# Attention blocks: V held in the array, P streaming for two heads on two column halves, row sums multiplied into the turned gate

## What is computed

```
for l in range(DEPTH):                       # DEPTH = 2
    u = rms_norm(x, g_pre[l]) @ w_in[l]
    (qa, ka, va, ga, qb, kb, vb, gb, rb, qm, gm) = split(u)
    oa = merge(moba_attention(q=8 heads of 64, k, v=va)) * silu(ga)   # causal, with ALiBi
    ob = merge(rms_norm(gla_attention(...), g_gla_out[l])) * silu(gb) # 4 heads, gated linear
    om = merge(mem_attention(q=4 heads of 64, mk, mv)) * silu(gm)     # 256 memory tokens
    x = x + concat([oa, ob, om]) @ w_out[l]
# mem_attention, and moba_attention for one block of 256 keys:
p = softmax(q @ k.T * scale + bias)          # 256 queries x 256 keys
o = p @ v                                    # 256 x 64 for each head
```

## Time and profile before

| | |
|---|---|
| median of 3 runs | 1408.54 us |
| profiled execution | 1409.29 us, span 1407.4 us |
| TensorE matmul busy | 1387.6 us, 99% |
| TensorE weight loads (beside matmuls) | 1142.5 us, 81% |
| VectorE busy | 1027.5 us, 73% |
| ScalarE busy | 1013.5 us, 72% |
| granted TensorE clock, mean | 0.999 |
| all DMA | 240.35 MB, 171 GB/s |

### The profile page before, as it was taken

One profiled execution on the slowest core, in us unless ns is written; L12 is line 12 of the kernel. 1 busy time (PEld: TensorE's weight loads), 2 busy tenths in 40 slices (PEclk: granted clock), 3 DMA queues, 4 the chain that ended last, 5 costly groups with the idle time before them and its releaser, 6 DMA issues.

```text
span 1407.4 us, 20632 instructions
## 1 busy us (share of the span) xinstructions
PE 1387.6 (99%) x7843; PEld 1142.5 (81%) x7843; DVE 1027.5 (73%) x1427; ACT 1013.5 (72%) x1838; POOL 74.8 (5%) x174
## 2 busy tenths in 40 slices
PE   7999999999999999999999999999999999999998
PEld 6788888888888888788887888887778888788886
DVE  5888788777666767776667766667988876876665
ACT  7657574748878555688785978767888886587784
POOL 8000000000000011000000000001120300000000
PEclk9999999999999999999999999999999999999999
DMA  7533453345656566556565656545453432566562
GB/s 233 192 120 94 150 194 122 119 150 181 202 186 205 181 227 209 184 191 204 184 202 172 202 187 198 191 154 194 144 149 123 110 123 91 168 209 203 185 206 91
DMA packets 168962, 240.35 MB, mean 171 GB/s; under 512 B 21714, under 2 KB 114800, under 8 KB 168864
## 3 DMA queue, kind: packets, MB, share of 16 engines
q1 hardware_dynamic: 166496, 233.57, 50.9%
q0 software_dynamic: 2336, 5.46, 1.4%
q10 hardware_dynamic: 32, 0.01, 0.0%
HBM read 236.12 MB, written 2.88 MB: 170 GB/s over the span
## 4 chain that ended last, share of the span: by engine, by line
PE 94%; DVE 2%; ACT 2%; DMA 1%; issue 0%; SPq 0%; ACTq 0%; DVEq 0%
PE A L261 18%; PE A L262 17%; PE A L263 17%; PE G L262 5%; PE M L262 5%; PE M L261 5%; PE M L263 5%; PE G L263 5%; PE G L261 5%; PE A L1349 1%; PE G L1270 1%; PE G L1317 1%; PE M L1327 1%; DMA block_cat<-in_mem 1%; DVE x_lo L439 1%; DVE tmp L434 1%
## 5 line engine op out<-in xcount | busy, mean ns | idle before, releaser
L243 DVE TENSOR_TENSOR w_lo<-raw,w_hi 128x1024 fp32r<-128x1024 f32 (+2 forms) x296 | 506.9, 1726 | 122.0 <-ACT w_hi L225 121.2
L225 ACT ACTIVATE w_hi<-raw 128x1024 fp32r<-128x1024 f32 (+2 forms) x296 | 427.2, 1462 | 116.1 <-DMA raw<-in_ffn_w_gate_up 86.9
L261 PE MATMUL A<-w_hi,x_hi 128*128 128x512 f32 (+1 forms) x640 | 258.2, 403 | 3.0 <-DVE x_lo L439 1.6
L263 PE MATMUL A<-w_hi,x_lo 128*128 128x512 f32 (+1 forms) x640 | 246.9, 386 | 0.0
L262 PE MATMUL A<-w_lo,x_hi 128*128 128x512 f32 (+1 forms) x640 | 246.8, 386 | 0.0
L714 ACT ACTIVATE ffn_ffn_hT<-ffn_ffn_hb 32x128 f32<-32x128 f32 x576 | 176.9, 307 | 15.7 <-DVE ffn_ffn_hb L779 2.5
L261 PEld LDWEIGHTS A<-w_hi,x_hi 128*128 128x128 f32 x640 | 120.3, 188 | 32.5 <-DVE x_lo L439 7.0
L263 PEld LDWEIGHTS A<-w_hi,x_lo 128*128 128x128 f32 x640 | 120.2, 188 | 25.1
L261 PE MATMUL A<-w_hi,ffn_ffn_hT_hi 128*128 128x512 f32 x352 | 138.1, 392 | 0.0
L262 PEld LDWEIGHTS A<-w_lo,x_hi 128*128 128x128 f32 x640 | 120.5, 188 | 21.0 <-issue 0.7
L262 PE MATMUL A<-w_lo,ffn_ffn_hT_hi 128*128 128x512 f32 x352 | 137.1, 389 | 0.0
(11 more groups left out here) (406 smaller groups left out, 2025.2 us busy)
## 6 DMA issues: line engine op xcount, KB each, us to landing
raw<-in_ffn_w_gate_up SPq DMA_DIRECT2D x176, 512.0 KB, 4.6
raw<-in_ffn_w_down SPq DMA_DIRECT2D x88, 512.0 KB, 3.9
raw<-in_w_in SPq DMA_DIRECT2D x48, 512.0 KB, 4.5
raw<-in_gdn_w_in SPq DMA_DIRECT2D x48, 512.0 KB, 4.5
raw<-in_sc_w_in SPq DMA_DIRECT2D x24, 512.0 KB, 4.5
raw<-in_w_out SPq DMA_DIRECT2D x16, 512.0 KB, 4.4
raw<-in_gdn_w_out SPq DMA_DIRECT2D x16, 512.0 KB, 4.0
raw<-in_w_mem_kv SPq DMA_DIRECT2D x8, 512.0 KB, 5.2
```

Of the source, the lines that this page charges most:

```text
L225: ins = act.activation(net.w_hi[:, v % RING, part], net.raw[:, v % RING, part], ACT.Copy)
L243: ins = dve.tensor_tensor(net.w_lo[:, v % RING, part], net.raw[:, v % RING, part], net.w_hi[:, v % RING, part].bitcast(F32), ALU.subtract)
L261: pe.matmul(out, xh, hi[:, k, c, :], start=start and k == 0, stop=False)
L263: mm = pe.matmul(out, xl, hi[:, k, c, :], start=False, stop=stop and k == nk - 1)
```

## The change

**P·V is turned round** (`pvp:n`, for heads n and n+1). V (128 keys x 64 columns) is now the stationary operand and PT streams, 256 tokens for the first 128 keys, and for the other 128 keys 128 tokens (causal heads) or 256 (memory heads). Head n uses the left 64 columns of the array, head n+1 the right 64 (`tile_position`), so O comes out transposed, features on the partitions, two heads in one 128-row block. `PT` gets four slots, which lie over QE and KE.

**The row sums go into the gate.** O can't be scaled by a row factor in this layout, so `jscale:g` multiplies the reciprocals into the gate, which still has tokens on the partitions; `gturn:g` transposes that part of the gate into a bank M. `ocopy:g` (ScalarE) copies O out of A[3] into the free part of `cat`, `join:g` (VectorE) multiplies it by the turned gate into `cT`, `join:g` on ScalarE copies the high part, `jlo:g` on VectorE the rest. `cturn` 0, 1 and 3 are gone, and three `gturn` come. Both tables are written anew around these steps.

```diff
-    unit:ga:0:3 pv:10 pturn:0 lo:16:0 join:1 hi:17:1 pv:11 scores:2 pturn:1 gate2:m
-    unit:ga:1:0 jgate:1
+    unit:ga:0:3 pturn:0 lo:16:0 hi:17:1 pvp:10 ocopy:1 scores:2 pturn:1 gate2:m
+    unit:ga:1:0 jscale:1
 ...
+        self.PT = [m[:, 2 * i:2 * i + 2, :].rearrange("p k t -> p (k t)") for m in (self.QE, self.KE) for i in range(2)]
+        self.oT = [self.cat[:, i, 0:512] for i in range(2)]
+        self.cT = self.cat[:, :, 768:1024]
 ...
             n = self.misc_no(step)
             if n >= 2 and self.misc[n - 2][0] == "cturn":
-                pe.wait_ge(*self.cat_lo(self.cturns.index(self.misc[n - 2]) + 1))
+                pe.wait_ge(*self.cat_lo(1))
+            elif n >= 2 and self.misc[n - 2][0] == "gturn":
+                pe.wait_ge(*self.joined(self.gturns.index(self.misc[n - 2]) + 1))
 ...
                 for b in range(3 if n < HEADS_A else 4):
-                    mm = pe.transpose(bank[:, b * P:(b + 1) * P], self.Pb[:, i % 3, b * P:(b + 1) * P],
+                    to = b if n < HEADS_A else b % 2 * 2 + b // 2
+                    mm = pe.transpose(bank[:, to * P:(to + 1) * P], self.Pb[:, i % 3, b * P:(b + 1) * P],
 ...
+            elif kind == "pvp":
+                n = int(step[1])
+                i = self.item_no(n)
+                g, kk = i // 4 + 1, i // 2 % 2
+                if i % 4 == 0:
+                    pe.wait_ge(*self.o_free(g))
 ...
+                for kt in range(2):
+                    lo = first if kt else 0
+                    for one in range(2):
+                        if kt == 0:
+                            pe.wait_ge(*self.is_free(("pturn", str(n + one))))
+                        mm = pe.matmul(net.A[3][HD * one:HD * (one + 1), kk * T + lo:(kk + 1) * T],
+                                       v[:, kt, at + HD * one:at + HD * (one + 1)],
+                                       self.PT[(i + one) % 4][:, kt * T:(kt + 1) * T - lo],
+                                       start=kt == 0, stop=kt == 1, tile_position=(0, HD * one))
+                if i % 4 == 2:
+                    mm.then_inc(self.pv_done.sem, 1)
 ...
+            elif kind == "gturn":
+                g = int(step[1])
+                bank = take_misc(step)
+                at = self.group_cols(g).start
+                pe.wait_ge(*self.gate_scaled(g))
+                for kk in range(2):
+                    for tt in range(TT):
+                        mm = pe.transpose(bank[:, kk * T + tt * P:kk * T + (tt + 1) * P],
+                                          self.gate[:, tt, at + kk * P:at + (kk + 1) * P], ident[:, :])
                 mm.then_inc(self.misc_done.sem, 1)
 ...
+            elif kind == "ocopy":
+                g = int(step[1])
+                act.wait_ge(*self.pv_done(g + 1))
+                act.activation(self.oT[g % 2], net.A[3][:, :], ACT.Copy).then_inc(self.o_free.sem, 1)
+            elif kind == "join":
 ...
+                act.wait_ge(*self.joined(g))
+                act.activation(self.catT_hi[grp][:, at:at + 2, :], self.cT, ACT.Copy).then_inc(self.cat_hi.sem, 1)
 ...
+            elif kind == "jscale":
 ...
                 dve.wait_ge(*self.probs(i0 + 4))
                 w.chain(dve.reciprocal(self.rr[:, :, i0:i0 + 4], self.rs[:, :, i0:i0 + 4]))
                 for tt in range(TT):
+                    part = self.gate[:, tt, self.group_cols(g)].rearrange("p (h d) -> p h d", d=HD)
+                    ins = dve.tensor_tensor(part, part, self.rr[:, tt, i0:i0 + 4].unsqueeze(2).to_broadcast([P, 4, HD]),
+                                            ALU.mult)
 ...
+                ins.then_inc(self.gate_scaled.sem, 1)
+            elif kind == "join":
+                g = int(step[1])
+                m = self.misc_no(("gturn", step[1]))
                 dve.wait_ge(*self.o_free(g + 1))
+                dve.wait_ge(*self.misc_done(m + 1))
+                dve.tensor_tensor(self.cT, self.oT[g % 2].rearrange("p (k t) -> p k t", k=2),
+                                  net.M[m % 2][:, :].rearrange("p (k t) -> p k t", k=2), ALU.mult)                   .then_inc(self.joined.sem, 1)
+                dve.wait_ge(*self.joined(g))
+            elif kind == "jlo":
 ...
+                dve.wait_ge(*self.cat_hi(g))
+                dve.tensor_tensor(self.catT_lo[grp][:, at:at + 2, :], self.cT,
+                                  self.catT_hi[grp][:, at:at + 2, :].bitcast(F32), ALU.subtract)                   .then_inc(self.cat_lo.sem, 1)
```

More of the change, by code:

```diff
@@ L975 @@
     unit:va:1:2 norm1:ka
-    unit:va:1:3 hi:16:1 norm2:ka lo:15:0 pv:8 pturn:10 lo:15:1
-    unit:ga:0:0 evac:va gfin pv:9 turn:ka0 lo:16:0 turn:qa1 pv:10 pturn:11 hi:17:0 scores:0 turn:ka1
+    unit:va:1:3 hi:16:1 norm2:ka lo:15:0 pturn:10 lo:15:1
+    unit:ga:0:0 evac:va gfin pvp:8 turn:ka0 lo:16:0 turn:qa1 pturn:11 hi:17:0 scores:0 turn:ka1
     unit:ga:0:1
     unit:ga:0:2 gate2:m
-    unit:ga:0:3 lo:16:1 join:1 pturn:0 pv:11 hi:17:1 scores:2 pturn:1
-    unit:ga:1:0 jgate:1
-    unit:ga:1:1 lo:17:0 cturn:2 evac:ga
-    unit:ga:1:2
-    unit:ga:1:3 pv:0 cturn:3 pturn:2 pv:1 hi:18:0 gate1:a gate_ln gate_exp lo:17:1 scores:4 pturn:3 hi:18:1
+    unit:ga:0:3 lo:16:1 pturn:0 pvp:10 ocopy:1 hi:17:1 scores:2 pturn:1
+    unit:ga:1:0 jscale:1
+    unit:ga:1:1 lo:17:0 cturn:2 evac:ga gturn:1
+    unit:ga:1:2 join:1 jlo:1
+    unit:ga:1:3 pvp:0 pturn:2 hi:18:0 gate1:a gate_ln gate_exp lo:17:1 scores:4 pturn:3 hi:18:1
     out:0:1:0
     out:0:1:1
-    out:0:1:2 pv:2 hi:19:0 pturn:4 hi:19:1 gate2:a scores:6
-    out:0:1:3 pv:3 pturn:5 join:2
-    out:1:1:0
-    out:1:1:1 jgate:2 pv:4 lo:18:0 lo:18:1 pturn:6 cturn:0 pv:5 lo:19:0 pturn:7 pv:6 hi:20:0 join:3 pv:7 jgate:3
+    out:0:1:2 pvp:2 ocopy:2 hi:19:0 pturn:4 hi:19:1 gate2:a scores:6
+    out:0:1:3 jscale:2 pturn:5
+    out:1:1:0 gturn:2
+    out:1:1:1 join:2 jlo:2 pvp:4 lo:18:0 lo:18:1 pturn:6 lo:19:0 pturn:7 jscale:3 gturn:3 pvp:6 ocopy:3 hi:20:0 join:3 jlo:3
     out:0:0:0
-    out:0:0:2 cturn:1
+    out:0:0:2
     out:1:1:2
@@ L1347, in pe @@
-                for tt in range(TT):
-                    for kt, b in enumerate(blocks[tt]):
-                        mm = pe.matmul(O[:, tt * T + at:tt * T + at + HD], pt[:, b * P:(b + 1) * P],
-                                       v[:, kt, cols], start=(kt == 0), stop=(b == blocks[tt][-1]))
-                if i % 4 == 3:
+                    v, at, first = self.y["va"], HD * n, P
+                else:
+                    v, at, first = self.y["mem"], 256 + HD * (n - HEADS_A), 0
+                for kt in range(2):
[7 more added lines that the diff above has]
+                                       start=kt == 0, stop=kt == 1, tile_position=(0, HD * one))
```

93 lines of the change are left out of this document (43 added, 50 removed).

## The result

The changed kernel took 1416.91 us (median of 4 runs, 1415.91 to 1418.33), the kernel before 1408.22. The ratio on record is 1.0042, with a 95% interval of 1.0028 to 1.0056; it isn't the quotient of the two medians, which is 1.0062. Forecast was 1411.5 and "no change that can be told"; it is slower, by 4 to 8 us as the interval has it. The profiled execution took 1416.41, 7.12 more than that of before.

The account below looks back on a forecast made before the run. TensorE, busy 99% of the span, was taken to bound the kernel: 1409.3 - 7.1 (cheaper P·V) + 9.3 (new waits) = 1411.5 us, 0.2% slower and no change that can be told; range 1405.5 to 1418.0.

Parts of the forecast that it names:

- What P·V costs after: P·V on TensorE, both layers: 0.71 us per pair of the first eight heads, 0.93 per memory pair, 9.4 in all; saved 7.1.
- the row-tile drains: Low end of the P·V saving: pairs at 0.95 and 1.16 us, 12.2 in all, so 4.2 us saved.
- Overlap of the halves: P·V pairs: the two column halves of the array run side by side, streaming 0.64 us per pair, 0.86 per memory pair.
- half-overlap: Rival, 12%: only neighbouring passes of a P·V pair overlap; saved 4.6 us, waits 8.7, 1413.4 us in all.
- The three named waits: New TensorE waits: last gturn of layer 2, 3.7 us; pvp:2 of layer 2, 1.7; last gturn of layer 1, 1.9.
- The small waits: Some eight places in both layers (gturn:1, gturn:2, turns of P), 0.1 to 0.6 us each, taken as 2.0 in sum.
- The clock: Rival, 10%: behind 3.7 us of standing TensorE could fall to 1.2 GHz, costing 2 to 6 us; 1415 us.
- TensorE's busy time: Sign in the profile after: TensorE's busy time falls by 7 us while its idle time grows by 9.
- The direction that I gave 36%: Whole kernel slower by over 0.3% (4.2 us), chance 0.36; within that bound 0.55, faster 0.09.
- the serial rival: Rival, 15%: a P·V pair's halves run one behind the other; P·V loses 1.2 us, waits 6.8, 1417.3 us.

## Why the prediction was off

By its sum the change was to cost 9.3 - 7.1 = 2.2 us. Between the marks it cost 7.9.

- **What P·V costs after: the step that failed.** I set a pair at "0.95 - 0.18 - 0.05 = 0.71 and 1.16 - 0.18 - 0.05 = 0.93", because "a column tile doesn't drain". It does: 0.95 and 1.16, the figures with the row-tile drains, which I had set down only as an end of the range. The row behind the choice was real but of another kind, a one-pass transpose, and I took it for a rule on column tiles. Start to start, with the entry and the exposed load behind, one layer's P·V takes 8.66 us before (I had 8.24; the change to the scores behind two of the heads is in it) and 5.99 after. Saved: 5.3 for both layers, not 7.1. Wrong by 1.8. The rule of the Trainium skill that I had weighed and left ("TensorEngine Tiling (Array Packing)", Key Properties: a change of tiling mode drains the engine) describes P·V; I priced it at 12 x 0.18, the runs at 12 x 0.30. One-pass instructions escaped it in the runs above.
- **Overlap of the halves.** Right, full. The other page of the Trainium skill that I cited ("TensorE: Matmul & The Clock Gate", Why this matters for your kernels), that separate column groups run concurrently, is borne out: starts 6 ns apart, 0.80 us for 1.28 of streaming. Serial and half-overlap rivals together had 27%, and neither came; exchanging the loops changed nothing in the overlap.
- **The three named waits.** Right. Last gate turn of layer 2: 3.7 forecast, 3.72. Last of layer 1: 1.9, and 1.62 listed (1.82 from start to start). pvp:2 of layer 2: 1.7, and 1.0 listed (1.66 between the starts of its two heads). Laying out VectorE's chain by durations of before was enough.
- **The small waits.** 2.0 forecast, 3.3 from start to start: 0.50 and 0.58 in layer 1 (a matmul of 512 columns behind a turn, gturn:2), and in layer 2 0.70 and 0.68 (gturn:2, gturn:1), 0.52 and 0.30 (turns of P and what follows). All waits: 10.6 instead of 9.3. The list shows 8.5, as each entry counts from a modelled end that is some 0.17 late, and the overlap that pvp:2 loses isn't in it.
- **The clock.** A rival at 10% with 2 to 6 us. It happened in both profiles of the changed kernel and cost 2.4 in the first. This was a term that the likeliest sum put at nothing: a stand of 3.7 us cost 6.1. The earlier trace rows showed such a case; I read it as the kernel's start, not as a rule for this place.
- **Sum.** -5.3 + 10.6 + 2.4 = 7.7; 0.2 of the 7.9 is left without an owner.
- **TensorE's busy time.** It was to fall by 7 and fell by 1.1. Only 5.3 were saved, and the 2.4 us at the low clock and the late modelled ends are booked as busy. So this sign says less than it seems to.

The direction that I gave 36% came. The range held, but not by its reasons: its upper end was set by the serial rival with its 1417.3, and that the measured 1416.91 lies beside it is chance, since the halves do overlap. Each of the three errors, 1.8, 1.3 and 2.4, went the same way.

## What to carry to other kernels

Price a stand of TensorE as the wait and what runs behind it at half rate; here 3.7 us became 6.1, and about 5.2 where the clock was low for a shorter time. Take the price of a mode change from an instruction of the same kind, passes included: a neighbour that is alike in shape only can mislead. And before giving up a rewrite that moves the order, look at what it waits for: here the same instructions in another order turned +0.4% into -0.4%.

## What the runs showed of the hardware beyond that

- Two-pass fp32 matmuls on part of the array (32 or 64 columns) lose about 0.30 us for each stay between full-array work; one-pass transposes and fp32r matmuls of the same widths lose nothing (0.33 us for two full transposes and one of either between them). How many passes an instruction has and what kind it is weren't told apart.
- Matmuls for different column halves start 13 ns apart even when all of one half's stand ahead in the queue. When the second half's operand is late the pair stretches (1.45 us instead of 0.80), and no wait is listed.
- The granted clock fell to 0.5 behind each of five stands of 3.7 us, behind one of three of 2.6 to 2.8, one of six of 1.6 and the one of 1.94, and not when the 3.7 us were filled with transposes.
